# The tile loop of an encoder kernel's front: order of the vector work, half-row copies a step later, list entries stored last

## The chip, the cores and the metric

The kernel runs on one core of a Trainium2 chip. The metric is the device time of one execution in microseconds; the number of a kernel is the median of its runs. The profile is one further execution, read with the hardware profiler.

## What is computed

The reference is one layer of a streaming encoder, for 1024 prompt tokens and 64 sample tokens of width 1024. What matters here is its beginning:

```
m = silu(c) @ w_ada + b_ada                 # (6 * 1024) values for each of 2 conditions
sh1, sc1, g1, sh2, sc2, g2 = split(m, 6)
h = rmsnorm(x, norm_mix) * (1 + sc1) + sh1  # 1088 x 1024
qa, ka, va, fa, qb, kb, vb = split(h @ w_in)
logf = log_sigmoid(fa + b_f)                # fa: 8 columns, the forget gates
```

Then come two groups of attention heads, an output projection, a router (top group, top two experts in it), 32 experts and a final norm. `w_ada` is 1024 x 6144, 24 MB; all of it has to be read for the two vectors `c` of the conditions.

## The kernel before

The kernel is a row of blocks: the front (`modulate_in`), attention, the output projection with the router, and the experts. In a block each engine runs an instruction list of its own, written out by hand; engines wait for each other by semaphores, and every engine has to leave a block before any enters the next. So the front lasts as long as its slowest engine.

**What the front does.** It cuts `w_ada` into 12 halves of 512 columns (2 MB each), numbered 0 to 11. It handles halves 0 to 8, and attention 9 to 11. Halves 0 to 3 give the shift and scale that the front itself needs; they come ahead of the tile loop. A half takes three steps: TensorE multiplies it by the two condition vectors (`partial_rows`, L244; the prediction calls it the product), ScalarE copies the result out of PSUM (`modulation_out`, L380), and TensorE sums and transposes the copy into columns (`summed_columns`, L448; "sums"). Two PSUM banks and two copies take turns: product n waits for the copy of n-2, and copy n waits for the sums of n-2.

**The tile loop.** The tokens are 9 tiles (eight of 128 and one of 64). For a tile t:
- ScalarE squares and sums the rows (`square`, L373), VectorE scales the sum (`mean_square`, L520), GpSimd raises it to the power -1/2 (L350), VectorE multiplies the rows by it (`normalise`, L525)
- TensorE transposes the tile, 8 transposes (`transpose_x`, L459)
- ScalarE (L389) and VectorE (L534) each `move` four of the eight blocks out of PSUM, with shift and scale applied
- ScalarE rounds the result to the high half (`upper`, L397), and VectorE takes what is left as the low half (`lower`, L542). Two buffers `h` take turns, so the moves of tile t wait for the lower of t-2

The transposes run two tiles ahead of the moves, the normalisation three, the squares four. In turn t of the loop TensorE also does a product (half 4 in turn 2, up to half 8 in turn 6) and the sums of the half of the turn before, and ScalarE copies that turn's product in the same turn, behind the square.

**The forget gates.** The columns of `fa` are made in three chunks of tokens, 0 to 383, 384 to 767 and 768 to 1087: `gate_part` (16 matmuls, L470) after turns 4 and 7 and at the end, a copy by ScalarE (L404), `gate_sum` (L477), and the logits with the bias on VectorE (L557, L555). One PSUM bank serves all three.

**Loads.** SP issues everything on one queue. Three halves have homes; half n waits until the product of the half that was last in its home is done. So half 7 waits for product 4, half 8 for product 5, half 9 for 6 and half 10 for 7. Behind half 6 SP also issues the first weights of attention (`raw`, L334) and the two stores that fill the router's list of entries with "no entry" (L337, L338), taken from `far`, the last of nine rows of a buffer. SP waits for these stores at the end of its block. GpSimd splits the raw weights into two halves (L354, L356) at the end of its list.

Of the kernel before, what the change touches and what calls it, by code (L numbers as in the profile page):

```python
# [25 lines left out]
P = 128  # L26
D = 1024
# [125 lines left out]
def build(nc, a, o):  # L153
    with ExitStack() as ctx:
# [35 lines left out]
        with ExitStack() as c0:  # L190
            both = Scope(nc, c0, "both")
            k["wide"] = both.sb("wide", [P, 4 * BAND])
            k["w_ld"] = [both.sem(f"w_ld{j}") for j in range(HELD)]
            k["mrow_ready"], k["mrow_out"] = both.sem("mrow_ready"), both.sem("mrow_out")
            k["mod_ready"], k["mod_out"] = both.sem("mod_ready"), both.sem("mod_out")
            with ExitStack() as c:  # L196
                s = Scope(nc, c, "in")
                modulate_in(nc, s, a, o, k, hT, w_split)
                k["past"] = s.sems
            with ExitStack() as c:  # L200
                attention(nc, Scope(nc, c, "att"), a, o, k, hT, w_split)
# [46 lines left out]
def modulate_in(nc, s, a, o, k, hT, w_split):  # L248
# [1 line left out]
    h_hi, h_lo = hT  # L250
    TILES = NT + 1
    AHEAD = 3
    X_FIRST = False
    w_ada = [k["rows_all"][:, 4 * j:4 * j + 4, :].rearrange("p t (a n) -> p (t a) n", a=2) for j in range(2)]
    w_ada += [s.sb("w_ada", [P, NC, D // 2])[:, :, :]]
    far = k["rows_all"][:, NT, :].bitcast(I32)
# [21 lines left out]
    sq_done, ms_done, rstd_done, xn_done = s.sem("sq_done"), s.sem("ms_done"), s.sem("rstd_done"), s.sem("xn_done")  # L278
    xT_ready, xT_out_act, xT_out_dve = s.sem("xT_ready"), s.sem("xT_out_act"), s.sem("xT_out_dve")
    hi_done, lo_done, wf_split = s.sem("hi_done"), s.sem("lo_done"), s.sem("wf_split")  # L280
    half_set, far_set, sc_clear, far_stored = s.sem("half_set"), s.sem("far_set"), s.sem("sc_clear"), s.sem("far_stored")
    f_ready, f_moved, f_summed, z_done = s.sem("f_ready"), s.sem("f_moved"), s.sem("f_summed"), s.sem("z_done")
    own_dve, w_hi_done, w_lo_done = s.sem("own_dve"), s.sem("w_hi_done"), s.sem("w_lo_done")
    xp, xs = a["x_prompt"][0], a["x_sample"][0]
    block = s.ctx.enter_context(nc.Block())
    FIRST = 4

    def halves_at(t):

        n = FIRST + t - 2  # L290
        return [n] if FIRST <= n < min(EARLY, HALVES - HELD) else []

    IN_LOOP = sum(len(halves_at(t)) for t in range(TILES))

    def chunk_ending(t):

# [2 lines left out]
    @block.sync  # L299
    def _(sp):  # L300
        def load_half(n):
            sp.dma_start(w_ada[W_HOME[n]], a["w_ada"][n]).then_inc(w_ld[W_HOME[n]], 16)

        def load_x(t):
            sp.dma_start(x[0:rows_of(t), t, :], xs if t == NT else xp[t * P:t * P + P, :]).then_inc(x_ld[t], 16)

        sp.dma_start(vecs[:, :], a["vecs"]).then_inc(vec_ld, 16)
        if X_FIRST:
            for t in range(2):
                load_x(t)  # L310
            sp.dma_start(consts[:, :], a["consts"][:, 0:K_END]).then_inc(c_ld, 16)
            for t in range(2, TILES):
                load_x(t)
            for n in range(HELD):
                load_half(n)
        else:
            load_half(0)
            sp.dma_start(consts[:, :], a["consts"][:, 0:K_END]).then_inc(c_ld, 16)
            for n in range(1, HELD):
                load_half(n)  # L320
            for t in range(3):
                load_x(t)
        for n in range(HELD, min(EARLY + 2, HALVES)):
            sp.wait_ge(mrow_ready, last_in_home(n) + 1)
            load_half(n)
            if n == HELD and not X_FIRST:
                for t in range(3, TILES):
                    load_x(t)
            if n == 4:
                sp.dma_start(w_f[:, :, :], a["w_f"]).then_inc(wf_ld, 16)  # L330
                sp.dma_start(b_f[:, :], a["b_f"]).then_inc(wf_ld, 16)
            if n == 6:
                sp.wait_ge(xT_ready, 3)
                sp.dma_start(raw, a["w_qkv"][0].rearrange("b p k n -> p b k n")).then_inc(raw_ld, 16)  # L334
                sp.wait_ge(far_set, 1)
                entries = k["lists"].rearrange("(p n) c -> p (n c)", p=P)
                sp.dma_start(entries[:, 0:D], far).then_inc(far_stored, 16)  # L337
                sp.dma_start(entries[:, D:LISTS // P * 4], far[:, 0:LISTS // P * 4 - D]).then_inc(far_stored, 16)  # L338
        sp.wait_ge(far_stored, 32)

    @block.gpsimd
    def _(pool):
# [17 lines left out]
    def _(act):  # L360
# [5 lines left out]
        def square(t):  # L366
            r = rows_of(t)
            m = min(t, NT - 1)
            unused = h_lo[0:r, :, m * P:m * P + P]
            if t == NT:  # L370
                act.wait_ge(sq_done, NT)
            act.wait_ge(x_ld[t], 16)
            act.activation(unused, x[0:r, t, :].rearrange("p (c n) -> p c n", c=NC), ACT.Square,  # L373
                           accum_out=ssq[0:r, t:t + 1]).then_inc(sq_done, 1)
# [28 lines left out]
                act.wait_ge(f_summed, c)  # L403
            act.activation(f_parts[:, 0:hi - lo], f_ps[:, 0:hi - lo], ACT.Copy).then_inc(f_moved, 1)  # L404

        if X_FIRST:
            for t in range(TILES):
                square(t)
            for n in range(FIRST):
                modulation_out(n)  # L410
        else:
            for n in range(FIRST - 1):
                modulation_out(n)
            for t in range(AHEAD):
                square(t)
            modulation_out(FIRST - 1)
            square(AHEAD)
        act.wait_ge(a1_done, 1)
        for t in range(TILES):
            move(t)  # L420
            upper(t)
            if t + AHEAD + 1 < TILES and not X_FIRST:
                square(t + AHEAD + 1)
            if t == 2:
                act.wait_ge(wf_ld, 32)
                act.activation(w_f_parts[:, :, 0:8], w_f[:, :, :], ACT.Copy).then_inc(wf_split, 1)
            for n in halves_at(t):
                modulation_out(n)
            if chunk_ending(t - 1) is not None:
                gate_rows_out(chunk_ending(t - 1))  # L430
        for n in range(FIRST + IN_LOOP, EARLY):
            modulation_out(n)
        gate_rows_out(2)

# [1 line left out]
    def _(pe):  # L436
# [25 lines left out]
        def gate_part(c):  # L462
            lo, hi = CHUNKS[c]
            pe.wait_ge(wf_split, 2)
            pe.wait_ge(lo_done, (hi + P - 1) // P)
            if c:
                pe.wait_ge(z_done, c)
            for i, part in enumerate((h_hi, h_lo)):
                for kc in range(NC):
                    ins = pe.matmul(f_ps[0:16, 0:hi - lo], w_f_parts[:, kc, :], part[:, kc, lo:hi],  # L470
                                    start=(i == 0 and kc == 0), stop=(i == 1 and kc == NC - 1))
            ins.then_inc(f_ready, 1)

        def gate_sum(c):
# [4 lines left out]

        pe.wait_ge(c_ld, 16)  # L480
        pe.wait_ge(silu_done, 1)
        if X_FIRST:
            transpose_x(0)
            transpose_x(1)
        partial_rows(0)
        for n in range(1, FIRST):
            if n == FIRST - 1 and not X_FIRST:
                transpose_x(0)
                transpose_x(1)
            partial_rows(n)  # L490
            summed_columns(n - 1)
        summed_columns(FIRST - 1)
        pe.wait_ge(a1_done, 1)
        for t in range(TILES):
            if t + 2 < TILES:
                transpose_x(t + 2)
            for n in halves_at(t):
                partial_rows(n)
            if chunk_ending(t - 1) is not None:
                gate_sum(chunk_ending(t - 1))  # L500
            for n in halves_at(t - 1):
                summed_columns(n)
            if chunk_ending(t) is not None:
                gate_part(chunk_ending(t))
        for n in halves_at(NT):
            summed_columns(n)
        for n in range(FIRST + IN_LOOP, EARLY):
            partial_rows(n)
            summed_columns(n)
        gate_part(2)  # L510
        gate_sum(2)
# [2 lines left out]
    def _(dve):  # L514
# [41 lines left out]
            end = min(hi, SEQ)  # L556
            dve.tensor_scalar(z[:, lo:end], f_ps[0:8, 0:end - lo], b_f[:, 0:1], None, ALU.add).then_inc(z_done, 1)  # L557

        ready = TILES if X_FIRST else AHEAD
        mean_square(0)  # L560
        for t in range(ready):
            if t + 1 < TILES:
                mean_square(t + 1)
            normalise(t)
# [4 lines left out]
        dve.wait_ge(a1_done, 1)  # L569
        for t in range(TILES):  # L570
            move(t)
            if t + ready < TILES:
                if t + ready + 1 < TILES:
                    mean_square(t + ready + 1)
                normalise(t + ready)
            if t:
                lower(t - 1)
            if t == 3:
                dve.wait_ge(wf_split, 1)
                dve.tensor_tensor(w_f_parts[:, :, 8:16], w_f[:, :, :], w_f_parts[:, :, 0:8], ALU.subtract)\  # L580
                   .then_inc(wf_split, 1)
            if t >= 2 and chunk_ending(t - 2) is not None:
                logits(chunk_ending(t - 2))
# [34 lines left out]
def attention(nc, s, a, o, k, hT, w_parts):  # L618
# [473 lines left out]
    def _(dve):  # L1092
# [124 lines left out]
        for n in range(ALL):  # L1217
            for at in range(TILES):
# [9 lines left out]
                if at == 1 and n + 1 < ALL:  # L1228
                    cache_lower(n + 1)
                    if n == 0:  # L1230
                        dve.wait_ge(pT_ready, turn["gates"] + 1)
                        dve.tensor_copy(gate_rows, pT_ps[turn["gates"] % 2][0:GATE_ROWS, 0, :]).then_inc(pT_out, 1)
                t, r, _, _, u = tile(n, at)
# [1052 lines left out]
```

## Time and profile before

| | us |
|---|---|
| median of 3 runs | 1245.49 |
| the runs | 1245.49, 1238.99, 1247.1 |
| the profiled execution | 1240.19 |
| its span, first to last instruction | 1238.4 |
| TensorE busy | 1100.7 (89%) |
| VectorE busy | 491.6 (40%) |
| ScalarE busy | 356.3 (29%) |
| GpSimd busy | 366.4 (30%) |
| mean granted clock of TensorE | 0.955 |

PE is TensorE's matmuls, PEld its weight loads, DVE VectorE, ACT ScalarE, POOL GpSimd, SP the queue engine. The page divides the span into 40 slices of 31 us; the front is the first two and nearly all of the third. In a timeline a row is one instruction or several of a line run together: start, duration, engine, line, operation, what it writes and reads, how many, and in brackets how long the engine had been idle before it and what ended that.

### The profile page before, as it was taken

What the parts mean: (1) busy time and instruction counts of PE and PEld (TensorE: products, weight loads), DVE (VectorE), ACT (ScalarE), POOL (GpSimd) and SP (SyncE); (2) the same over time, 40 slices, a digit from 0 to 9 for tenths busy, and PEclk for the clock granted to TensorE, in tenths of its full rate; (3) what the DMA queues carried; (4) which work ended last, traced back from release to release, by engine and by line L of the source; (5) the groups of instructions that cost most, each with busy time, mean ns of one, the idle gap of its engine ahead of it and who ended that gap; (6) DMA issues with size and microseconds to landing.
All of it is one profiled execution on the core that took longest, in us unless ns stands there. A gap on an engine that the chain in (4) does not pass through costs nothing. (4 is left out here: it accounts for less than half of the span.)

```text
span 1238.4 us, 20082 instructions
## 1 busy us (share of the span) xinstructions
PE 1100.7 (89%) x7180; PEld 767.1 (62%) x7180; DVE 491.6 (40%) x1307; ACT 356.3 (29%) x1130; POOL 366.4 (30%) x306
## 2 busy tenths in 40 slices
PE   5589999999999899999986899962999999989956
PEld 2348788888888788888875688851333333333322
DVE  0453344444444344453555267754111212111227
ACT  2643334434334334433454122210111111011102
POOL 1150633535353403113033144435222222121001
PEclk8799999999999999999999899975999999999978
DMA  9953323223141504021077511125999999999784
GB/s 382 404 196 110 96 69 108 93 64 101 62 118 34 166 1 120 14 72 45 1 221 212 188 69 69 69 103 215 398 374 373 413 414 393 406 368 422 281 306 158
DMA packets 86809, 238.63 MB, mean 193 GB/s; under 512 B 10456, under 2 KB 58024, under 8 KB 75952
## 3 DMA queue, kind: packets, MB, share of 16 engines
q1 hardware_dynamic: 68384, 132.01, 30.5%
q10 hardware_dynamic: 7344, 78.91, 15.8%
q0 software_dynamic: 10976, 26.32, 5.7%
q8 instruction: 65, 1.06, 0.3%
q14 instruction: 40, 0.33, 0.1%
HBM read 208.19 MB, written 38.45 MB: 199 GB/s over the span
## 5 line engine op out<-in xcount | busy, mean ns | idle before, releaser
L1987 PE MATMUL moe_gu_ps<-a_gu,moe_xT_sb 128*64 x416 | 185.1, 598 | 5.2 <-DMA b_gu<-in_w_gu 3.3
L942 PE MATMUL att_piece_ps<-hT_hi,w_hi 128*128 128x384 f32 (+1 forms) x528 | 184.4, 349 | 2.4 <-PEq L196 1.0
L1990 PE MATMUL moe_gu_ps<-b_gu,moe_xT_sb 128*64 128x512 f32 x416 | 185.1, 598 | 0.0
L942 PE MATMUL att_piece_ps<-hT_hi,w_lo 128*128 128x384 f32 (+1 forms) x528 | 172.7, 327 | 0.0
L942 PE MATMUL att_piece_ps<-hT_lo,w_hi 128*128 128x384 f32 (+1 forms) x528 | 172.5, 327 | 0.0
L1167 DVE COPY att_pT_sb<-att_pT_ps 128x512 f32<-128x512 f32 (+2 forms) x192 | 94.6, 520 | 133.4 <-PE att_pT_ps L1010 132.9
L1987 PEld LDWEIGHTS moe_gu_ps<-a_gu,moe_xT_sb 128*64 128x64 f32 x416 | 57.0, 138 | 125.7 <-issue 125.7
L1271 ACT ACTIVATE att_probs_sb<-att_probs_sb,att_nmax_sb 128x640 f32<-128x640 f32 (+5 forms) x144 | 101.4, 704 | 41.3 <-DVE att_nmax_sb L1153 40.6
L1289 ACT ACTIVATE keep_rows_all_sb<-att_o_ps,att_rden_sb 128x64 f32<-128x64 f32 x144 | 37.3, 310 | 246.8 <-PE att_o_ps L1031 246.8
L942 PEld LDWEIGHTS att_piece_ps<-hT_hi,w_hi 128*128 128x128 f32 x528 | 99.1, 188 | 11.1 <-issue 6.0
L1153 DVE CUSTOM_DVE_ANT_0 att_probs_sb<-att_s_ps,both_wide_sb 128x640 f32<-128x640 f32 (+5 forms) x144 | 95.3, 662 | 26.8 <-PE att_s_ps L998 15.0
L2010 PE MATMUL moe_y_ps<-a_dn,moe_hT_sb 128*64 x208 | 94.8, 598 | 5.4 <-DVE moe_hT_sb L2156 4.7
L942 PEld LDWEIGHTS att_piece_ps<-hT_lo,w_hi 128*128 128x128 f32 x528 | 99.5, 188 | 0.0
L942 PEld LDWEIGHTS att_piece_ps<-hT_hi,w_lo 128*128 128x128 f32 x528 | 99.1, 188 | 0.0
L2013 PE MATMUL moe_y_ps<-b_dn,moe_hT_sb 128*64 128x512 f32 x208 | 94.8, 598 | 0.0
L1010 PE MATMUL att_pT_ps<-keep_consts_sb,att_probs_sb 128*128 128x128 f32 (+2 forms) x560 | 87.7, 278 | 1.8 <-ACT att_probs_sb L1271 1.7
L907 POOL CAST w_hi<-att_w_raw_sb 128x1024 fp32r<-128x1024 f32 x21 | 21.8, 1039 | 212.2 <-PE att_piece_ps L942 173.6
L1025 PE MATMUL att_o_ps<-att_pT_sb,att_v_rows_sb 128*64 128x128 f32 (+1 forms) x1088 | 74.4, 277 | 7.7 <-DVE att_pT_sb L1167 6.5
L1931 POOL DMA_INDIRECT x<-h_rows,moe_entries_sb x26 | 25.8, 993 | 161.6 <-DMA moe_entries_sb<-lists,route_at_sb 75.5
L1010 PEld LDWEIGHTS att_pT_ps<-keep_consts_sb,att_probs_sb 128*128 128x128 f32 (+2 forms) x560 | 62.7, 139 | 16.9 <-issue 11.6
L1025 PEld LDWEIGHTS att_o_ps<-att_pT_sb,att_v_rows_sb 128*64 128x64 f32 (+1 forms) x1088 | 58.1, 136 | 23.2 <-issue 13.2
L2073 ACT ACTIVATE moe_xT_sb<-moe_xT_ps 128x512 f32<-128x512 f32 x26 | 15.5, 598 | 187.9 <-PE moe_xT_ps L1976 183.7
(312 smaller groups left out, 1964.1 us busy)
## 6 DMA issues: line engine op xcount, KB each, us to landing
b_gu<-in_w_gu ACTq DMA_DIRECT2D x25, 2048.0 KB
b_dn<-in_w_dn ACTq DMA_DIRECT2D x25, 1024.0 KB
a_gu<-in_w_gu SPq DMA_DIRECT2D x10, 2048.0 KB
keep_rows_all_sb<-in_w_ada SPq DMA_DIRECT2D x9, 2048.0 KB, 11.2
att_w_raw_sb<-in_w_qkv SPq DMA_DIRECT2D x21, 512.0 KB, 3.7
a_dn<-in_w_dn SPq DMA_DIRECT2D x10, 1024.0 KB
w_out_parts<-keep_rows_all_sb SPq DMA_DIRECT2D x16, 512.0 KB, 4.8
in_w_ada_sb<-in_w_ada SPq DMA_DIRECT2D x3, 2048.0 KB, 16.6
```

The source lines that it names most:

```text
L942: ins = pe.matmul(bank[:, 0:hi - lo], w[:, kind, kc, :], x[:, kc, lo:hi], start=(m == 0), stop=(m == 3 * NC - 1))
L1010: ins = pe.transpose(pT_ps[e % 2][0:m, b - b0, 0:r], probs[h][0:r, b * P:b * P + m], ident[0:r, 0:r])
L1025: ins = pe.matmul(o_ps[head, 0:r], v, pT[h][0:m, b, 0:r], start=(b == 0), stop=(b == len(kb) - 1))
L1153: dve.tensor_tensor_reduce(probs[h][0:r, 0:wide], s_ps[h][0:r, 0:wide], bias, -SCALE, BIG, ALU.add, ALU.min, nmax[0:r, 2 * at + h:2 * at + ...
L1167: ins = dve.tensor_copy(pT[h][:, b0:b1, :], pT_ps[e % 2][:, 0:b1 - b0, :])
L1271: act.activation(probs[h][0:r, 0:wide], probs[h][0:r, 0:wide], ACT.Exp, bias=nmax[0:r, 2 * at + h:2 * at + h + 1], scale=-1.0, accum_out=d ...
L1289: ins = act.activation(rows_all[0:r, t, first + HD * h:first + HD * h + HD], o_ps[0:r, P + HD * h:P + HD * h + HD], ACT.Copy, scale=rden[0 ...
L1931: pool.indirect_dma_start(x[p % 3][:, :], None, k["h2"], bass.IndirectOffsetOnAxis(ap=entry[:, p, 0:1], axis=0), bounds_check=TOK - 1, oob ...
L1987: pe.matmul(gu_ps[p % 2][LANE[0], :], xT[:, c, LANE[0]], a_gu[:, bass.ds(slot, 1), c, :].rearrange("p a n -> p (a n)"), start=(c == 0), st ...
L1990: ins = pe.matmul(gu_ps[p % 2][LANE[1], :], xT[:, c, LANE[1]], b_gu[p % 3][:, c, :], start=(c == 0), stop=(c == NC - 1))
L2010: pe.matmul(y_ps[LANE[0], half], hT[:, c, LANE[0]], a_dn[:, bass.ds(slot, 1), c, half].rearrange("p a n -> p (a n)"), start=(c == 0), stop ...
L2013: ins = pe.matmul(y_ps[LANE[1], half], hT[:, c, LANE[1]], b_dn[p % 2][:, c, half], start=(c == 0), stop=(c == 1))
```

## The change

- VectorE's order in a turn is now moves, lower, normalise, mean square; it was moves, mean square, normalise, lower.
- The products of halves 4 to 8 are in turns 2, 3, 4, 6 and 8 (they were in 2 to 6). ScalarE copies a product in the turn after it, and TensorE makes the sums in the turn after that (in a turn, before gate part and gate sum).
- SP issues the stores of the list entries at the end of its list, behind half 10, and no longer waits for them. VectorE waits for them in attention, before it overwrites a part of that row.
- The last gate part is two sets of 16 matmuls, over tokens 768 to 1023 and 1024 to 1087, the first without a wait for the lower of the last tile.
- A branch for another order of loads, switched off by a constant, is removed.

```diff
@@ modulate_in
+    HALF_AT = {2: 4, 3: 5, 4: 6, 6: 7, 8: 8}
     def halves_at(t):
-        n = FIRST + t - 2
-        return [n] if FIRST <= n < min(EARLY, HALVES - HELD) else []
-    IN_LOOP = sum(len(halves_at(t)) for t in range(TILES))
+        return [HALF_AT[t]] if t in HALF_AT else []
@@ SP, inside "if n == 6" before, behind the loop after
-                sp.wait_ge(far_set, 1)
-                entries = k["lists"].rearrange("(p n) c -> p (n c)", p=P)
-                sp.dma_start(entries[:, 0:D], far).then_inc(far_stored, 16)
-                sp.dma_start(entries[:, D:LISTS // P * 4], far[:, 0:LISTS // P * 4 - D]).then_inc(far_stored, 16)
-        sp.wait_ge(far_stored, 32)
+        sp.wait_ge(far_set, 1)
+        entries = k["lists"].rearrange("(p n) c -> p (n c)", p=P)
+        sp.dma_start(entries[:, 0:D], far).then_inc(k["far_stored"], 16)
+        sp.dma_start(entries[:, D:LISTS // P * 4], far[:, 0:LISTS // P * 4 - D]).then_inc(k["far_stored"], 16)
@@ ACT
         for t in range(TILES):
             move(t)
             upper(t)
-            if t + AHEAD + 1 < TILES and not X_FIRST:
+            if t + AHEAD + 1 < TILES:
                 square(t + AHEAD + 1)
...
-            for n in halves_at(t):
+            for n in halves_at(t - 1):
                 modulation_out(n)
             if chunk_ending(t - 1) is not None:
                 gate_rows_out(chunk_ending(t - 1))
-        for n in range(FIRST + IN_LOOP, EARLY):
+        for n in halves_at(TILES - 1):
             modulation_out(n)
         gate_rows_out(2)
@@ PE, gate_part(c)
             pe.wait_ge(wf_split, 2)
-            pe.wait_ge(lo_done, (hi + P - 1) // P)
             if c:
                 pe.wait_ge(z_done, c)
-            for i, part in enumerate((h_hi, h_lo)):
-                for kc in range(NC):
-                    ins = pe.matmul(f_ps[0:16, 0:hi - lo], w_f_parts[:, kc, :], part[:, kc, lo:hi],
-                                    start=(i == 0 and kc == 0), stop=(i == 1 and kc == NC - 1))
+            for n0, n1 in [(lo, min(hi, SEQ))] + [(SEQ, hi)] * (hi > SEQ):
+                pe.wait_ge(lo_done, (n1 + P - 1) // P)
+                for i, part in enumerate((h_hi, h_lo)):
+                    for kc in range(NC):
+                        ins = pe.matmul(f_ps[0:16, n0 - lo:n1 - lo], w_f_parts[:, kc, :], part[:, kc, n0:n1],
+                                        start=(i == 0 and kc == 0), stop=(i == 1 and kc == NC - 1))
@@ PE, the loop
                 transpose_x(t + 2)
             for n in halves_at(t):
                 partial_rows(n)
-            if chunk_ending(t - 1) is not None:
-                gate_sum(chunk_ending(t - 1))
-            for n in halves_at(t - 1):
+            for n in halves_at(t - 2):
                 summed_columns(n)
             if chunk_ending(t) is not None:
                 gate_part(chunk_ending(t))
-        for n in halves_at(NT):
-            summed_columns(n)
-        for n in range(FIRST + IN_LOOP, EARLY):
-            partial_rows(n)
+            if chunk_ending(t - 1) is not None:
+                gate_sum(chunk_ending(t - 1))
+        for n in halves_at(TILES - 2) + halves_at(TILES - 1):
             summed_columns(n)
         gate_part(2)
         gate_sum(2)
@@ DVE, the loop
             move(t)
-            if t + ready < TILES:
-                if t + ready + 1 < TILES:
-                    mean_square(t + ready + 1)
-                normalise(t + ready)
             if t:
                 lower(t - 1)
+            if t + AHEAD < TILES:
+                normalise(t + AHEAD)
+            if t + AHEAD + 1 < TILES:
+                mean_square(t + AHEAD + 1)
@@ attention, DVE, pair 0, second tile
                     if n == 0:
+                        dve.wait_ge(k["far_stored"], 32)
                         dve.wait_ge(pT_ready, turn["gates"] + 1)
                         dve.tensor_copy(gate_rows, pT_ps[turn["gates"] % 2][0:GATE_ROWS, 0, :]).then_inc(pT_out, 1)
```

## Rows read from the trace of the kernel before

**Rows 1.** Page, 40 slices of the span: granted clock in tenths.
```profile
PEclk8799999999999999999999899975999999999978
```
**Rows 2.** Timeline of PE, the seam to attention: start, duration, idle before.
```profile
90.00 0.42 PE L942 MATMUL att_piece_ps<-hT_hi,w_hi 128*128 128x384 f32 x1 [1.02 <-PEq L196]
```
**Rows 3.** Waits, 30 to 92 us: total, times, longest.
```profile
ACT both_wide_sb L380 <- PE in_row_ps L244: 20.7, 6, 5.7
```
**Rows 4.** Timeline of ACT, turn 3 of the tile loop.
```profile
51.84 1.50 ACT L389 ACTIVATE in_h_sb<-in_xT_ps,keep_mod_sb,in_a_sb 128x128 f32<-128x128 f32 x4
53.37 1.06 ACT L397 ACTIVATE hT_hi<-in_h_sb 128x1024 fp32r<-128x1024 f32 x1
54.34 1.04 ACT L373 ACTIVATE hT_lo<-in_x_sb 128x1024 fp32r<-128x1024 f32 x1
...
58.07 0.60 ACT L380 ACTIVATE both_wide_sb<-in_row_ps 128x512 f32<-128x512 f32 x1 [2.60 <-PE in_row_ps L244]
```
**Rows 5.** Timeline of PE, 46 to 88 us.
```profile
46.30 1.94 PE L459 MATMUL in_xT_ps<-keep_consts_sb,in_x_sb 128*128 128x128 f32 x8 [3.79 <-ACT in_h_sb L389]
...
53.44 1.42 PE L459 MATMUL in_xT_ps<-keep_consts_sb,in_x_sb 128*128 128x128 f32 x8 [2.17 <-ACT in_h_sb L389]
54.79 3.20 PE L244 MATMUL in_row_ps<-in_w_ada_sb,both_wide_sb 128*32 128x512 f32 x16
...
65.56 1.55 PE L470 MATMUL in_f_ps<-hT_hi,in_w_f_parts_sb 128*16 128x384 f32 x8
...
68.35 1.03 PE L459 MATMUL in_xT_ps<-keep_consts_sb,in_x_sb 128*128 128x128 f32 x8
69.31 1.92 PE L244 MATMUL in_row_ps<-keep_rows_all_sb,both_wide_sb 128*32 128x512 f32 x16
72.31 0.81 PE L477 MATMUL in_f_ps<-in_f_parts_sb,keep_consts_sb 16*8 16x384 f32 x2 [1.08 <-ACT in_f_parts_sb L404]
73.05 1.05 PE L448 MATMUL in_mod_ps<-keep_consts_sb,both_wide_sb 128*128 128x2 f32 x8
74.03 0.82 PE L459 MATMUL in_xT_ps<-keep_consts_sb,in_x_sb 64*128 64x64 f32 x8
74.78 3.44 PE L244 MATMUL in_row_ps<-in_w_ada_sb,both_wide_sb 128*32 128x512 f32 x16
...
86.43 1.34 PE L470 MATMUL in_f_ps<-hT_lo,in_w_f_parts_sb 128*16 128x320 f32 x8
```
**Rows 6.** Timeline of DVE: first moves, a lower, a normalise, the last logits.
```profile
34.66 1.37 DVE L534 TENSOR_SCALAR in_h_sb<-in_xT_ps,in_a_sb,keep_mod_sb 128x128 f32<-128x128 f32 x4
...
49.09 1.22 DVE L542 TENSOR_TENSOR hT_lo<-in_h_sb,hT_hi 128x1024 fp32r<-128x1024 f32 x1
...
55.58 0.74 DVE L525 TENSOR_SCALAR in_x_sb<-in_x_sb,in_rstd_sb 128x1024 f32<-128x1024 f32 x1
...
89.22 0.46 DVE L557 TENSOR_SCALAR both_wide_sb<-in_f_ps,in_b_f_sb 8x256 f32<-8x256 f32 x1
```
**Rows 7.** DMA issues at 17.6, 24.4, 31.8, 38.4, 51.3 us: KB, us to landing.
```profile
keep_rows_all_sb<-in_w_ada SPq DMA_DIRECT2D x1, 2048.0 KB, 24.9
...
in_w_ada_sb<-in_w_ada SPq DMA_DIRECT2D x1, 2048.0 KB, 23.2
...
keep_rows_all_sb<-in_w_ada SPq DMA_DIRECT2D x1, 2048.0 KB, 20.6
...
lists<-keep_rows_all_sb SPq DMA_DIRECT2D x1, 512.0 KB, 17.9
...
keep_rows_all_sb<-in_w_ada SPq DMA_DIRECT2D x1, 2048.0 KB, 11.2
```
**Rows 8.** Windows: PE, PEld, DVE, ACT, POOL busy; clock, DMA share, GB/s.
```profile
76.00:77.00 1.00, 1.00 (x8) 0.20 (x4) 0.89 (x4) 0.00 (x0) 1.00 (x1) 0.50 1.00 426
...
84.00:86.00 2.00, 1.21 (x8) 1.00 0.00 0
```
**Rows 9.** Timeline of DVE in attention, the copy behind the new wait.
```profile
152.05 0.27 DVE L1232 COPY keep_rows_all_sb<-att_pT_ps 64x128 f32<-64x128 f32 x1
```

More of the change, by code:

```diff
@@ L194, in build @@
             k["mrow_ready"], k["mrow_out"] = both.sem("mrow_ready"), both.sem("mrow_out")
-            k["mod_ready"], k["mod_out"] = both.sem("mod_ready"), both.sem("mod_out")
+            k["mod_ready"], k["mod_out"], k["far_stored"] = both.sem("mod_ready"), both.sem("mod_out"), both.sem("far_stored")
             with ExitStack() as c:
@@ L252, in modulate_in @@
     AHEAD = 3
-    X_FIRST = False
     w_ada = [k["rows_all"][:, 4 * j:4 * j + 4, :].rearrange("p t (a n) -> p (t a) n", a=2) for j in range(2)]
@@ L280, in modulate_in @@
     hi_done, lo_done, wf_split = s.sem("hi_done"), s.sem("lo_done"), s.sem("wf_split")
-    half_set, far_set, sc_clear, far_stored = s.sem("half_set"), s.sem("far_set"), s.sem("sc_clear"), s.sem("far_stored")
+    half_set, far_set, sc_clear = s.sem("half_set"), s.sem("far_set"), s.sem("sc_clear")
     f_ready, f_moved, f_summed, z_done = s.sem("f_ready"), s.sem("f_moved"), s.sem("f_summed"), s.sem("z_done")
@@ L307, in _ @@
         sp.dma_start(vecs[:, :], a["vecs"]).then_inc(vec_ld, 16)
[L308 to L322, printed above, removed]
+        load_half(0)
+        sp.dma_start(consts[:, :], a["consts"][:, 0:K_END]).then_inc(c_ld, 16)
+        for n in range(1, HELD):
+            load_half(n)
+        for t in range(3):
+            load_x(t)
         for n in range(HELD, min(EARLY + 2, HALVES)):
@@ L325, in _ @@
             load_half(n)
-            if n == HELD and not X_FIRST:
+            if n == HELD:
                 for t in range(3, TILES):
@@ L404, in gate_rows_out @@
             act.activation(f_parts[:, 0:hi - lo], f_ps[:, 0:hi - lo], ACT.Copy).then_inc(f_moved, 1)
[L406 to L417, printed above, removed]
+        for n in range(FIRST - 1):
+            modulation_out(n)
+        for t in range(AHEAD):
+            square(t)
+        modulation_out(FIRST - 1)
+        square(AHEAD)
         act.wait_ge(a1_done, 1)
@@ L481, in _ @@
         pe.wait_ge(silu_done, 1)
-        if X_FIRST:
-            transpose_x(0)
-            transpose_x(1)
         partial_rows(0)
         for n in range(1, FIRST):
-            if n == FIRST - 1 and not X_FIRST:
+            if n == FIRST - 1:
                 transpose_x(0)
@@ L557, in logits @@
             dve.tensor_scalar(z[:, lo:end], f_ps[0:8, 0:end - lo], b_f[:, 0:1], None, ALU.add).then_inc(z_done, 1)
-        ready = TILES if X_FIRST else AHEAD
         mean_square(0)
-        for t in range(ready):
+        for t in range(AHEAD):
             if t + 1 < TILES:
```

## The prediction

> **What bounds the kernel now.** The page first: the span is 1238.4 us, and the front is its first two to three slices of 31 us, the ones where TensorE was granted 0.8, 0.7 and 0.9 of its clock [rows 1]. The timeline of PE at the seam gives its end: attention's first matmul is at 90.00 us, once every engine has left the front's block [rows 2]. The change touches only what lies before that, so the question is how early 90.00 can come.
>
> The waits of 30 to 92 us say who is late there. ScalarE waits six times, 20.7 us in all, for PE's half-row products (L380 on L244) [rows 3], and TensorE idles 3.79 us before the transposes of tile 4 until ScalarE's move is done [rows 5]. Neither is slow; they wait for each other. The timeline of ACT shows the cycle: move of a tile 1.50 us, high half (upper) 1.06, square 1.04 and its read, then 2.60 us idle until PE's product exists, the copy of it 0.60 (0.5 before the next can start), and only then the next move, although that tile's transpose had long been there [rows 4]. On PE: transposes 1.42, product of a half 3.20, sums 1.05 [rows 5]. One turn is move 1.5, transposes 1.4, product 3.2, copy 0.5, handovers 0.1: 6.7 us, and from tile 2 to tile 7 it is paid each time. VectorE is not the limit: moves 1.37, lower 1.22, normalise 0.74 make 3.3 us a tile [rows 6].
>
> **The change, part by part.** I write the new order out by the waits in the code, with those durations, from 34.66 us, where both moves of tile 0 start [rows 6] and nothing ahead is touched. The same was done for the old order as a control: it comes out at 89.9 us for the last VectorE instruction, against 89.22 + 0.46 = 89.7 in the trace [rows 6].
>
> *Lower directly behind the moves.* Old, the lower of tile t-1 stood behind the scaled square sum and the normalisation, which wait for ScalarE's square. The old ACT move of tile 2 waited for it. New, a step is: upper 1.0, square 1.1, sum 0.1, VectorE's moves 1.3, handover: 3.6 to 3.7 us. ACT's move of tile 2 ends at 43.4 and PE's transposes of tile 4 run 43.5 to 45.4 (1.94 us [rows 5]). Old they started at 46.3. Gain here: about 2.7 us. The normalisation of tile t+3 comes later in its step, but is still 2 us or more ahead of its transpose. The square sum is last; it holds only the next moves, as it did before.
>
> *Copies a step later.* ScalarE now does the next move before it waits for the product, so move and product lie side by side. From 45.4 PE no longer waits for anybody; it becomes the bound: product 4 to 48.6, transposes 5 to 50.0, product 5 to 53.2, transposes 6 to 54.6, product 6 to 57.8, sums 4 to 58.8, gate part 0 (16 matmuls, two blocks of 1.55 that overlap: 3.0) to 61.8, transposes 7 (1.0) to 62.8, sums 5 to 63.8, gate sum 0 to 64.5, transposes 8 to 65.3, product 7 (1.9) to 67.2, sums 6 to 68.2, gate part 1 to 71.2, product 8 (3.4) to 74.6, sums 7 to 75.6, gate sum 1 to 76.3, sums 8 to 77.3 [rows 5]. ACT waits for gate part 0 before its move of tile 6 (62.2 to 63.7), and transposes 8 need that move: 0.8 us to spare, the tightest place. VectorE ends the lower of tile 8 at about 70.5.
>
> *The tail.* VectorE adds the bias rows (0.2) after sums 8 and makes logits 1 (0.6): 78.1. Gate part 2 waits for that, as before. Split, it is 16 matmuls of 256 columns and 16 of 64. Eight of 384 take 1.55 and eight of 320 take 1.34 [rows 5], so 64 columns are worth about 0.2: eight of 256 about 1.1, sixteen 2.1. For sixteen of 64 columns no row exists: between 0.8 (the slope) and 2.1 (no gain at all from being short); I take 1.0, near the slope. Together 3.1 against the 2.5 or so of two unsplit blocks: the split costs 0.6 us, and gives nothing, because the lower of tile 8 is done 7 us before. Then the ACT copy 0.4, gate sum 0.7 and logits 0.7: 83.2. The seam costs 0.3 as before (89.7 to 90.0): attention starts at 83.5 instead of 90.0. **6.5 us gained.**
>
> *SP and the loads.* Landings from issue [rows 7]: half 4 at 17.6 + 24.9 = 42.5, half 6 at 31.8 + 20.6 = 52.4, the list entries at 38.4 + 17.9 = 56.2, half 7 at 51.3 + 11.2 = 62.5. Half 5, at 24.4 + 23.2, is between: 47.5. Products 4, 5 and 6 start at 45.4, 50.0 and 54.6, so each has 2.2 to 3 us to spare. Half 7 is issued when product 4 is done (48.6 instead of 51.3). The 0.55 MB of entries, worth 1.3 us at 426 GB/s, as the loads run [rows 8], are no longer ahead of it: it lands at about 60.7, and is wanted at 65.3. Half 8 follows 5 us later (65.7, wanted at 71.2). The entries are now behind half 10, which is issued at 67.2 and lands by 76; they follow by 78, with the queue empty until 83.5. SP leaves its block without waiting for them. VectorE's new wait stands before the copy at 152.05 [rows 9], some 70 us after; cost nothing. Behind it on VectorE are reciprocals and the next pieces, so if the entries were late, all of attention would stop. GpSimd begins its split of the raw weights earlier (56 instead of 64.5), and needs 14 us: 70, covered.
>
> *The dead branch for the other load order* was never run: nothing.
>
> **Sum.** Profiled execution 1240.19 us (span 1238.4 and 1.8 around it) minus 6.5 is 1233.7. The three runs give 1238.99, 1245.49 and 1247.1, so the profiled one is 5.3 us under their median. The median less 6.5 is 1239.0. The two levels occur about equally often, so I take the middle, 1237. Attention's PE is busy nearly throughout and nothing in it is timed from the start of the program, so I expect the 6.5 us to arrive at the end undiminished.
>
> **The clock** is where my sum is weakest. Product 8 took 3.44 us and product 7 1.92 for the same work [rows 5]. At 76 to 77 us the granted clock is 0.50 (1.2 GHz) with PE busy 1.00 [rows 8]; before that PE had done sums of 2 columns and 64-column transposes, after a gap of 1.08 us [rows 5]. So in this trace a busy PE was slowed, and I left products 4, 5, 6 and 8 at the slow price.
> The Trainium skill (page "TensorE: Matmul & The Clock Gate", the clock-gate part) says that half rate is the state after idleness and full rate that after sustained activity. By it an unbroken PE from 43.5 on would run products 5, 6 and 8 at about 1.9 us, and the front would end at 79.2 and not 83.2. The 0.50 in a busy stretch speaks against taking that rule whole.
>
> **Rivals.**
> 1. *Full clock from product 5 on.* The mechanism is in this kernel: PE's gaps before the transposes, 3.79 us in the row of tile 4 [rows 5], go away, and the three products fall from 3.2 to 3.4 to 1.9. That is 1.3 + 1.3 + 1.5, on PE's unbroken chain: 4.0 more, less what half 6 at 52.4 may hold back. The gain is 10.5, the time 1229.7 to 1235. For: products 3 to 8 vary just so. Against: the row above. Chance 0.15.
> 2. *Half clock all through* (the slower side). From transposes 6 on, the chain is 28 us of PE. If the short matmuls kept the clock at 1.2 GHz there, products 7 would cost 1.4 more, five groups of sums 0.8 each, the gate parts 3.0, 3.0 and 3.1, transposes and gate sums 3: about 19 us, so the front would end at 102: 12.5 later than now, 1252.7 to 1258. It decides from about 6.5 us of such loss on. Against: the trace shows 0.50 for single stretches only, and 1.00 at 84 to 86 with PE busy 1.21 us of 2 [rows 8]. Chance 0.03.
> 3. *The time is given back.* PE stays bound by ACT at the gate rows: the copy of gate part 0 stands on ACT before the move of tile 6, so each delay of PE reaches the move and comes back to PE at transposes 8. With 0.8 us to spare, a product one clock step slower there is paid in full, and VectorE's lower, 1.2 us alone, stretches beside GpSimd's split. Gain 0 to 3 us: 1237 to 1245. Chance 0.14.
> 4. The forecast, gain 4 to 9 us: 0.68.
>
> **Numbers.** 1% is 12.4 us, about what can be told from no change here. The forecast gain is half that, so *same* holds most: 0.87. Faster needs rival 1 together with the lower level of the runs: 0.10. Slower: 0.03. The range: 1230.5 (the low level, gain 8.5) to 1243.5 (the high level, gain 2 to 3), which leaves out rival 2 and the ends of 1 and 3.
>
> **What would show it.** In the timeline of PE, products 4, 5 and 6 at about 45, 50 and 55 us with no idle from the transposes of tile 4 to sums 6; ACT's idle before L380 mostly gone; attention's first matmul at 83.5 (81 to 86). Gate part 2 in two blocks, 3.1 us. The entries' store landing near 78. The clock in the stretch 53 to 75. I am wrong if that first matmul is under 81 or over 87, or if the time between it and the end differs from 1148.4 us by more than 3.

## The result, and the profile after

The changed kernel takes 1231.46 us (median of 7 runs, 1230.81 to 1234.2), the kernel before 1241.63 beside it (7 runs, 1238.99 to 1247.54): ratio 0.991, interval 0.9889 to 0.9931. The time is inside the range of 1230.5 to 1243.5, at its lower edge, and 5.5 under the 1237 of the sum; the gain is 10.2 us where 6.5 were forecast.

The profiled execution (1234.2 us, one of the two longest of the seven) has a span of 1232.4. Two lines of its page, the span and the granted clock, to be read against [rows 1]:

```profile
span 1232.4 us, 20113 instructions
...
PEclk8789999999999999999998999975999999999978
```

The timeline of PE through the tile loop, rows as in [rows 5]:

```profile
43.48 1.94 PE L441 MATMUL in_xT_ps<-keep_consts_sb,in_x_sb 128*128 128x128 f32 x8 [1.73 <-DVE in_h_sb L511]
45.35 3.12 PE L244 MATMUL in_row_ps<-keep_rows_all_sb,both_wide_sb 128*32 128x512 f32 x16
48.41 1.09 PE L441 MATMUL in_xT_ps<-keep_consts_sb,in_x_sb 128*128 128x128 f32 x8
49.43 1.92 PE L244 MATMUL in_row_ps<-in_w_ada_sb,both_wide_sb 128*32 128x512 f32 x16
51.28 1.09 PE L441 MATMUL in_xT_ps<-keep_consts_sb,in_x_sb 128*128 128x128 f32 x8
52.31 1.92 PE L244 MATMUL in_row_ps<-keep_rows_all_sb,both_wide_sb 128*32 128x512 f32 x16
...
55.08 1.56 PE L453 MATMUL in_f_ps<-hT_hi,in_w_f_parts_sb 128*16 128x384 f32 x8
...
60.99 1.92 PE L244 MATMUL in_row_ps<-keep_rows_all_sb,both_wide_sb 128*32 128x512 f32 x16
...
66.64 1.92 PE L244 MATMUL in_row_ps<-in_w_ada_sb,both_wide_sb 128*32 128x512 f32 x16
...
72.12 1.86 PE L453 MATMUL in_f_ps<-hT_hi,in_w_f_parts_sb 128*16 128x256 f32 x8 [0.85 <-issue]
...
78.23 0.41 PE L918 MATMUL att_piece_ps<-hT_hi,w_hi 128*128 128x384 f32 x1 [1.03 <-PEq L196]
```

From 43.48 to 71.3 PE has no idle time worth a bracket. Transposes 4 start at 43.48, as worked out (43.5), and product 4 still takes 3.12 us. But products 5, 6 and 8 take 1.92 each; the forecast had 3.2, 3.2 and 3.4. Attention's first matmul is at 78.23 instead of 90.00 [rows 2]: 11.8 us earlier, not 6.5. The prediction had said what would show it wrong: a first matmul under 81, or a time from it to the end more than 3 us off 1148.4. Both came: 78.23, and 1232.4 - 78.23 = 1154.2.

ScalarE idled 2.60 us before the copy in the rows shown [rows 4], and 2.6 to 3.6 before each of the five. Now the copies of halves 4 to 7 come without a wait, and only that of half 8 waits 1.40 us (timeline of ACT, the copy at the end of turn 3 and the start of turn 4):

```profile
49.11 0.58 ACT L368 ACTIVATE both_wide_sb<-in_row_ps 128x512 f32<-128x512 f32 x1
49.59 1.50 ACT L377 ACTIVATE in_h_sb<-in_xT_ps,keep_mod_sb,in_a_sb 128x128 f32<-128x128 f32 x4
51.12 1.06 ACT L385 ACTIVATE hT_hi<-in_h_sb 128x1024 fp32r<-128x1024 f32 x1
```

The issues of SP at 48.5 and 51.4 us (half 7 and half 8), with the time to landing, as in [rows 7]:

```profile
keep_rows_all_sb<-in_w_ada SPq DMA_DIRECT2D x1, 2048.0 KB, 12.3
...
in_w_ada_sb<-in_w_ada SPq DMA_DIRECT2D x1, 2048.0 KB, 14.4
```

They land at 60.8 and 65.8 (forecast 60.7 and 65.7). Product 7 starts at 60.99, 0.2 us behind its half. TensorE got so much faster that it now runs level with the loads: a half 7 that lands any later holds it up.

**Of the 11.8 us, 6.0 arrive at the end of this execution** (1238.4 against 1232.4). VectorE's instructions in attention are the same ones in the same order in both kernels, so their distance can be followed: 10.2 us at 89 us of the changed kernel, 8.7 from 134 on, 7.4 from 440 on. Those are three steps of 1.3 to 1.6 us; smaller ones take the rest, among them two places where the clock is lower than before over the same work (mean 0.83 against 0.87 in the 40 us from 655, 0.72 against 0.77 in the 30 us from 1170; in the kernel before, from 664 and 1178). Windows of the changed kernel at those three places (columns: PE, PEld, DVE, ACT, POOL busy, clock, DMA share, GB/s):

```profile
80.00:82.00 2.00, 2.00 (x8) 2.00 (x8) 0.00 (x0) 1.06 (x2) 0.00 (x0) 0.51 0.39 128
130.00:132.00 2.00, 2.00 (x10) 1.78 (x11) 0.61 (x3) 0.60 (x2) 0.00 (x0) 0.50 0.87 238
420.00:422.00 2.00, 2.00 (x8) 2.00 (x7) 0.02 (x1) 0.10 (x2) 2.00 (x2) 0.50 0.00 0
```

At each, PE is fully busy at half clock, within 1 us behind a gap. The gaps are there in both kernels: 1.03 us at the seam (1.02 before), 1.70 at 129.5 (1.70) and 2.55 at 419 (2.78), and in the kernel before the clock stayed at 1.00 behind all three. The one at 129.5 is this, in the changed kernel and then in the one before:

```profile
129.52 0.33 PE L986 MATMUL att_pT_ps<-keep_consts_sb,att_probs_sb 128*128 128x128 f32 x1 [1.70 <-ACT att_probs_sb L1248]
```
```profile
139.75 0.33 PE L1010 MATMUL att_pT_ps<-keep_consts_sb,att_probs_sb 128*128 128x128 f32 x1 [1.70 <-ACT att_probs_sb L1271]
```

and the window behind the latter (PE busy, clock, DMA share, GB/s):

```profile
140.00:142.00 2.00, 2.00 (x15) 1.00 0.79 193
```

The same idle 1.70 us was followed by half clock once and not the other time. Twelve profiles stand in this document, and the program behind the front is the same in all but for one wait of VectorE. From attention's first matmul to the end they take 1148.2 to 1155.3 us: 1148.4 in the kernel before, 1154.2 and 1152.9 in two profiles of the changed one. So a difference of 6 us there is within what single executions differ by; over 7 runs each, the medians differ by 10.2 us.

### The profile page after: what moved, and what is told of

It reads as the page before. It is cut to its first block and busy times, and to the rows that moved or that the text cites. A ratio compares the mean times of both kernels' runs of the same rounds, so it can differ in the third digit from the quotient of the medians.

```text
span 1232.4 us, 20113 instructions
## 1 busy us (share of the span) xinstructions
PE 1102.8 (89%) x7196; PEld 772.9 (63%) x7196; DVE 492.3 (40%) x1307; ACT 355.8 (29%) x1130; POOL 363.6 (30%) x306
```

## The experiments

The measure of the front is attention's first matmul in the profile: before 90.0, changed 78.2. Each label names its edit.

**VectorE's order alone**, on the kernel before:

```diff
             move(t)
-            if t + ready < TILES:
-                if t + ready + 1 < TILES:
-                    mean_square(t + ready + 1)
-                normalise(t + ready)
             if t:
                 lower(t - 1)
+            if t + ready < TILES:
+                normalise(t + ready)
+            if t + ready + 1 < TILES:
+                mean_square(t + ready + 1)
```

> The kernel before with VectorE's new order alone (moves, lower, normalise, mean square). Attention's first matmul is the measure: 90.0 us in the kernel before, 78.2 in the changed one, a gain of 11.8. Theory A (two waits in series: each part alone leaves the other one on the path): the cycle of ScalarE and TensorE by the copy in the same turn stays, so the step of turns 3 to 6 stays at about 6.7 us, only turns 1 and 2 get shorter; first matmul at 87 (86 to 88), TensorE's clock still 0.5 in several stretches of 35 to 75 us. Rival B (the parts add up, and the order of the vector work is the larger one): 83 or earlier.

Measured: first matmul 87.34; ratio 0.9974 (0.9945 to 1.0003), not to be told from no change. The timeline of PE, turns 3 and 4:

```profile
50.77 1.43 PE L459 MATMUL in_xT_ps<-keep_consts_sb,in_x_sb 128*128 128x128 f32 x8 [2.17 <-issue]
52.13 3.20 PE L244 MATMUL in_row_ps<-in_w_ada_sb,both_wide_sb 128*32 128x512 f32 x16
...
57.50 1.32 PE L459 MATMUL in_xT_ps<-keep_consts_sb,in_x_sb 128*128 128x128 f32 x8 [1.19 <-issue]
58.75 3.29 PE L244 MATMUL in_row_ps<-keep_rows_all_sb,both_wide_sb 128*32 128x512 f32 x16
```

The step is 57.50 - 50.77 = 6.73, as before. The 2.7 us come from turns 1 and 2 alone, as the prediction had it.

**The copies alone** (products in turns 2, 3, 4, 6, 8; copies one turn, sums two turns later), on the kernel before:

```diff
+    HALF_AT = {2: 4, 3: 5, 4: 6, 6: 7, 8: 8}
...
@@ ACT
-            for n in halves_at(t):
+            for n in halves_at(t - 1):
                 modulation_out(n)
...
@@ PE
-            for n in halves_at(t - 1):
+            for n in halves_at(t - 2):
                 summed_columns(n)
...
```

> The kernel before with copies a step later, products in turns 2, 3, 4, 6 and 8 and the sums two turns later, but VectorE's old order, the list entries behind the raw weights and the last gate part in one piece. Theory A: ScalarE's moves now wait for the lower, which stands behind square sum and normalisation; written out by the waits this gives a first matmul at 87.5 at the half-clock prices of the kernel before and 84.5 at full clock. Rival B (this part is nearly all of it, by TensorE's unbroken work and its full clock): 79 to 80.

Measured: first matmul 84.81, in an execution whose tile loop began 1.4 us earlier in the span (transposes 2 at 35.03 against 36.4), so 86.2 on the scale of the others; ratio 0.9966 (0.9942 to 0.999). Product 5 is already at full clock here. The row of transposes 6 shows what is left: ScalarE's move is late, which waits for the lower.

```profile
50.62 1.06 PE L460 MATMUL in_xT_ps<-keep_consts_sb,in_x_sb 128*128 128x128 f32 x8 [0.73 <-ACT in_h_sb L390]
51.61 1.92 PE L244 MATMUL in_row_ps<-in_w_ada_sb,both_wide_sb 128*32 128x512 f32 x16
56.33 1.94 PE L460 MATMUL in_xT_ps<-keep_consts_sb,in_x_sb 128*128 128x128 f32 x8 [2.80 <-ACT in_h_sb L390]
58.20 2.52 PE L244 MATMUL in_row_ps<-keep_rows_all_sb,both_wide_sb 128*32 128x512 f32 x16
```

Alone the two parts bring 2.7 and 3.8 us in these profiles, and the whole change, with the entries moved as well, 11.8. That isn't yet a proof that they are worth more together. With both of them and the entries at their old place (below), the first matmul is at 83.97: 6.0 us earlier, no more than the sum of 6.5. And full clock doesn't need both: with the copies alone products 5, 7 and 8 took 1.92 us, product 5 behind a gap of 0.73, and only product 6, behind one of 2.80, took 2.52. The runs add up too: 0.3% for the order, 0.3% for the copies, 0.7% for both with the entries early, 0.9% for all, each uncertain by about 0.3%.

**Products in turns 2 to 6 again**, on the changed kernel:

```diff
-    HALF_AT = {2: 4, 3: 5, 4: 6, 6: 7, 8: 8}
+    HALF_AT = {2: 4, 3: 5, 4: 6, 5: 7, 6: 8}
```

> The changed kernel with the products of halves 4 to 8 in turns 2 to 6 again; the copies stay a step later. Theory A (the loads have become the bound: in the changed kernel product 7 starts at 60.99 with half 7 landed at 60.8): product 7 in turn 5 has to wait for its half until 60.8 with sums, gate sum and transposes behind it on TensorE, and product 8 until 65.8; first matmul at 80.8, 2.6 later than the changed kernel's 78.2. Rival (spreading is idle, the copy a step later is all): 78.2 as the changed kernel.

Measured: first matmul 79.49; ratio 0.9961 (0.9932 to 0.9989), 1230.76 to 1243.55 over 10 runs. The timeline of PE, and one long window of it (PE busy, clock, DMA share, GB/s):

```profile
60.96 1.92 PE L244 MATMUL in_row_ps<-keep_rows_all_sb,both_wide_sb 128*32 128x512 f32 x16 [1.93 <-DMA keep_rows_all_sb<-in_w_ada]
...
65.86 1.92 PE L244 MATMUL in_row_ps<-in_w_ada_sb,both_wide_sb 128*32 128x512 f32 x16 [0.61 <-DMA in_w_ada_sb<-in_w_ada]
...
74.73 1.09 PE L453 MATMUL in_f_ps<-hT_hi,in_w_f_parts_sb 128*16 128x256 f32 x8 [0.75 <-issue]
```
```profile
47.00:92.00 45.00, 39.78 (x295) 1.00 0.72 287
```

Both waits for loads are there; the loss is 1.3 us and not 2.6, since the last gate part ran at full clock here. A wait of 1.93 us right before product 7, the longest for a half in any profile here, cost no clock: it is 1.00 from 47 to 92 us. This profile is of the fastest run; with waits before the products the runs spread over 13 us, where the changed kernel's spread over 3.4 and 3.8. The slower runs have the lower mean clock over the whole program: 0.958 for the two runs at 1231 us, 0.948 to 0.952 for the six above 1237. So the clock has a part in the spread; whether it is lost in the front isn't shown, as no slower run was profiled.

**The entries behind the raw weights again**, on the changed kernel:

```diff
                 sp.dma_start(raw, ...).then_inc(raw_ld, 16)
-        sp.wait_ge(far_set, 1)
...
+                sp.wait_ge(far_set, 1)
...
+                sp.dma_start(entries[:, 0:D], far).then_inc(k["far_stored"], 16)
+                sp.dma_start(entries[:, D:LISTS // P * 4], ...).then_inc(k["far_stored"], 16)
```

> The changed kernel with the stores of the list entries issued behind the raw weights again (SP still doesn't wait for them). Theory A (loads bound product 7): half 7 lands 1.3 us later, product 7 starts about 1.2 us later, the first matmul is at 79.4 instead of 78.2. Rival (the entries are cover, as the prediction had it with 4 us of slack): 78.2, no change.

Measured: first matmul 83.97; ratio 0.9934 (0.9908 to 0.996). The timeline of PE, and one window of it (busy, clock, DMA share, GB/s):

```profile
62.36 3.64 PE L244 MATMUL in_row_ps<-keep_rows_all_sb,both_wide_sb 128*32 128x512 f32 x16 [1.25 <-DMA keep_rows_all_sb<-in_w_ada]
65.93 1.87 PE L430 MATMUL in_mod_ps<-keep_consts_sb,both_wide_sb 128*128 128x2 f32 x8
67.66 2.72 PE L453 MATMUL in_f_ps<-hT_hi,in_w_f_parts_sb 128*16 128x384 f32 x8
```
```profile
64.00:66.00 2.00, 2.00 (x13) 0.50 1.02 434
```

The load's delay is what was expected, 1.25 us. But product 7, the sums and most of gate part 1 behind it then ran at half clock: 5.7 us later in all. Both theories missed this. The wait alone doesn't explain it. In the kernel with products in turns 2 to 6, product 7 waited 1.93 us and stayed at full clock, and in the kernel with the last gate part in one piece (below) product 6 did so behind this wait:

```profile
52.27 1.92 PE L244 MATMUL in_row_ps<-keep_rows_all_sb,both_wide_sb 128*32 128x512 f32 x16 [1.29 <-DMA keep_rows_all_sb<-in_w_ada]
```

Over the runs this kernel is about 0.2% behind the changed one, within the intervals of both.

**The same, with the wait filled** by four useless matmuls ahead of product 7:

```diff
                 for n in halves_at(t):
+                    if n == 7:
+                        pe.wait_ge(mrow_out, n - 1)
+                        for _ in range(4):
+                            pe.matmul(row_ps[1][:, 0:384], ident, consts[:, 0:384], start=True, stop=True)
                     partial_rows(n)
```

> The kernel with the entries behind the raw weights (first matmul at 83.97, where product 7 waited 1.25 us for its half and then ran at half clock until about 72 us), with 4 useless matmuls of 384 columns put directly ahead of product 7, in the time in which it waits; they write a bank that product 7 overwrites. Theory A (the short gap, not the late load itself, costs most: it lets the clock fall): product 7 at full clock (1.9 us), first matmul at 79.5 to 80.0, 4 us or more earlier although work was added. Rival B (the clock fell by chance, or for the low use of the array by the sums): product 7 at 3.4 to 3.6 us as without them, first matmul at 84 or later.

The timeline of PE, and the same window:

```profile
61.04 2.85 PE L481 MATMUL in_row_ps<-keep_consts_sb 128*128 128x384 f32 x8
63.82 1.92 PE L244 MATMUL in_row_ps<-keep_rows_all_sb,both_wide_sb 128*32 128x512 f32 x16
```
```profile
64.00:66.00 2.00, 2.00 (x19) 1.00 0.96 410
```

Measured: first matmul 80.97. The fill was too long, product 7 started 1.5 us later than without it, and the front still ended 3.0 us earlier, at full clock until the last gate part. The ratio says less: 0.9945 (0.9919 to 0.9972), no better than unfilled. So one pair of profiles shows what the half clock cost, but not that the fill kept it away, since waits as long passed without it elsewhere, one of 1.53 us before product 6 in this same profile. The runs don't confirm a gain.

**The changed kernel again**, unedited:

> The changed kernel itself once more, beside the others. Theory A (TensorE's unbroken work from 43.5 us on holds the full clock up to the end of the front, so the front's end varies little; the stretches at half clock behind it fall where a sample hits a gap and differ from execution to execution): first matmul of attention at 78.2 plus or minus 0.5, runs again within about 5 us of each other, ratio 0.991 to 0.993. Rival (the profile of the first time was lucky in the front, and the rivals of the prediction at slow prices are as common): first matmul anywhere between 78 and 84.

Measured: 1233.05 us, ratio 0.9913 (0.9876 to 0.9951), runs 1231.97 to 1235.73. First matmul 79.62, 0.9 beyond the range expected and inside that of the rival. Products 5 to 8 take 1.92 or 1.93 again; in the timeline of PE the whole last gate part, its sum and the first matmuls of attention ran at half clock:

```profile
72.42 1.87 PE L453 MATMUL in_f_ps<-hT_hi,in_w_f_parts_sb 128*16 128x256 f32 x8 [0.85 <-issue]
74.09 1.91 PE L453 MATMUL in_f_ps<-hT_lo,in_w_f_parts_sb 128*16 128x256 f32 x8
```

**The last gate part in one piece**, on the changed kernel:

```diff
-            for n0, n1 in [(lo, min(hi, SEQ))] + [(SEQ, hi)] * (hi > SEQ):
+            for n0, n1 in [(lo, hi)]:
```

> The changed kernel with the last gate part in one piece (16 matmuls of 320 columns, waiting for the lower of the last tile, which is done 6 us before). Theory A: the split costs what it adds, 3.85 us in two pieces in the changed kernel against 2.5 to 2.7 in one; first matmul at 77.0 to 77.2, that is 1.0 to 1.2 earlier, if the clock is full there. Rival: the split's first piece starts earlier than one piece could, so undoing it costs: 78.5 or later.

Measured: first matmul 78.43; 1234.9 us, ratio 0.9926 (0.989 to 0.9961). Neither number was met, because here too most of the part fell into half clock (timeline of PE):

```profile
72.14 1.91 PE L453 MATMUL in_f_ps<-hT_hi,in_w_f_parts_sb 128*16 128x320 f32 x8 [0.85 <-issue]
73.86 2.33 PE L453 MATMUL in_f_ps<-hT_lo,in_w_f_parts_sb 128*16 128x320 f32 x8
```

At full clock the part takes 2.5 us split (the kernel with products in turns 2 to 6) and 2.5 in one (below). At half clock it takes 4.4 split (72.42 to 76.84, the kernel run again); the 4.05 in one can't be set against that, because its first 0.5 us were still at full clock. The split is worth nothing and costs nothing that shows.

**A denser end**, on the changed kernel with the gate part in one piece:

```diff
@@ PE
+            if t == NT:
+                gate_sum(1)
             for n in halves_at(t - 2):
                 summed_columns(n)
...
-            if chunk_ending(t - 1) is not None:
+            if chunk_ending(t - 1) is not None and t < NT:
                 gate_sum(chunk_ending(t - 1))
+        gate_part(2)
         for n in halves_at(TILES - 2) + halves_at(TILES - 1):
             summed_columns(n)
-        gate_part(2)
         gate_sum(2)
@@ DVE
+        logits(1)
         modulated(FIRST, EARLY).then_inc(k["mod_out"], 1)
-        logits(1)
         logits(2)
```

> The changed kernel with a denser end: gate sum 1 ahead of the sums of half 7, the last gate part in one piece and ahead of the sums of half 8, VectorE's logits 1 ahead of the bias rows. The waits of TensorE for VectorE (0.85) and for ScalarE's copy (0.5) then lie beside sums. Theory A (TensorE's own work is the bound behind product 8, which its load holds at 65.8): after product 8 (66.64 plus 1.9) come 0.7, 1.0, 2.6, 1.0 and 0.7 on TensorE and 0.7 on VectorE: first matmul at 75.5 (75 to 76.3), 2.7 earlier, of which half is the split. Rival (the wait moves on to ScalarE or to the logits): no better than the unsplit kernel, 77.0.

Measured: first matmul 75.19; 1228.17 us (4 runs, 1227.23 to 1229.88; the five runs of the changed kernel beside it are all above 1231.9), ratio to the kernel before 0.9863 (0.9827 to 0.99). Its slowest run is faster than the fastest of the twelve runs of the changed kernel (1230.81), so it beats both kernels. The timeline of PE from gate sum 1 on:

```profile
68.59 0.81 PE L460 MATMUL in_f_ps<-in_f_parts_sb,keep_consts_sb 16*8 16x384 f32 x2
69.33 1.05 PE L430 MATMUL in_mod_ps<-keep_consts_sb,both_wide_sb 128*128 128x2 f32 x8
70.24 1.33 PE L453 MATMUL in_f_ps<-hT_hi,in_w_f_parts_sb 128*16 128x320 f32 x8
71.42 1.33 PE L453 MATMUL in_f_ps<-hT_lo,in_w_f_parts_sb 128*16 128x320 f32 x8
```

The wait of 0.85 us ahead of the gate part is gone, and the part ran at full clock. That the wait was the cause isn't shown by this one profile. Of the seven profiles of a changed kernel with an idle 0.75 or 0.85 us there, six had half clock in some of the part and one had none; the kernel before, with 0.79, had none either.

**The idle time at the loop's start filled**, on the changed kernel:

```diff
+            if t < 3:
+                for _ in range(2):
+                    pe.matmul(row_ps[1][:, 0:384], ident, consts[:, 0:384], start=True, stop=True)
             if t + 2 < TILES:
                 transpose_x(t + 2)
```

> The changed kernel with two useless matmuls of 384 columns ahead of the transposes in each of turns 0, 1 and 2, where TensorE sits idle 1.5 to 2.8 us. If that brings the full clock earlier, product 4 takes 1.9 instead of 3.1 us and transposes 5 start 1.2 us earlier. Theory A (from product 7 on the loads are the bound; half 7 lands at 60.8 whatever TensorE does before): product 7 doesn't start before 60.8, first matmul at 78.0 to 78.5, no gain; and if the wait ahead of product 7 that opens costs the clock, 82 or later. Rival (TensorE's own work was the bound): first matmul at 77.0, 1.2 earlier.

Measured: 1232.28 us, ratio 0.9913 (0.9881 to 0.9946), the same as unfilled. Product 4 takes 1.92 and transposes 5 start at 47.29 instead of 48.41, and then, in the same timeline:

```profile
51.31 1.06 PE L441 MATMUL in_xT_ps<-keep_consts_sb,in_x_sb 128*128 128x128 f32 x8 [1.10 <-ACT in_h_sb L377]
52.45 1.92 PE L244 MATMUL in_row_ps<-keep_rows_all_sb,both_wide_sb 128*32 128x512 f32 x16
...
61.14 1.92 PE L244 MATMUL in_row_ps<-keep_rows_all_sb,both_wide_sb 128*32 128x512 f32 x16
```

The 1.1 us are given back before product 7: transposes 6 wait 1.10 us for ScalarE's move and start where they did (51.28), and half 6, issued at 31.9, takes 20.5 us and lands at 52.4, where product 6 starts. So product 7 is where it was (60.99), and its half, issued 2 us earlier than in the changed kernel, still lands only at 61.1. From product 6 on TensorE can't be earlier than the loads. The first matmul is at 79.62, again by half clock in the last gate part.

**Both**, the denser end and the filled start:

> Both: the denser end and the filled start. Theory A: first matmul at 75.2 as with the denser end alone (75.19), since half 7 sets product 7; the time no better than the denser end's 1228.2. Rival: 74.0.

Measured: 1228.93 us (8 runs), ratio 0.9899 (0.9872 to 0.9926): no better than the denser end alone. The first matmul was at 78.86, in an execution whose tile loop began 1.6 us later, and in which product 7 ran at half clock (3.59 us), behind transposes 8 and an idle 0.45 us before them. Filling the start doesn't protect the rest.

## Why the prediction was right or wrong

**The cycle of copy, move and transposes: right.** Transposes 4 were worked out at 43.5 (43.48), transposes 5 at 48.6 (48.41), with no idle after them. What the order does alone, 2.7 us, came out as forecast, and the step of 6.7 us stayed until the copies moved.

**The step that failed: "I left products 4, 5, 6 and 8 at the slow price".** Three of the four ran at full clock. Followed through the list, the measured start is earlier than the forecast one by 1.9 us at transposes 6, 3.6 at sums 4, 4.3 at product 7, 6.1 at sums 7; the products make up 4.0 of it, transposes 5 and 6 (1.09 against 1.4), the gate parts (2.8 against 3.0) and small roundings of the other terms the rest. The last gate part gave back 0.8, since it ran at half clock (3.9 us against 3.1). In all 5.3 us. The step went by rows of the kernel before, product 5 at 3.20 behind an idle 2.17 us and a busy TensorE at half clock at 76 us, and priced with them a stretch that had no gap at all. The row at 76 us came after sums, short transposes and a gap. What the runs showed in its place is the price, 1.92 us, in both profiles of the changed kernel. Why the clock is full there is shown only in part: it held through the unbroken stretch from 48.4 us on, but in other runs it also held with gaps.
Rival 1 had the front end at 79.2, attention at 79.5 and the time at 1229.7 to 1235; with 78.23 and 1231.46 it was the right case, and 0.15 was too little for it. That the time still fell in the stated range is the range's width and no merit of the sum: of the 5.5 us it was off, 3.7 are the gain, and the rest is that it took the kernel before at 1243.5 where seven runs gave 1241.63. The rule of the Trainium skill (page "TensorE: Matmul & The Clock Gate", the clock-gate part) that activity brings full rate and idleness half rate was the better guide: products 5 to 8 are at 1.92 us in the unbroken stretch in both profiles of the changed kernel, and 3.64 behind a wait of 1.25 us. Of short waits the traces don't agree on either answer: behind 1.29, 1.53 and 1.93 us a product took 1.92.

**The loads: landings right, conclusion wrong.** 60.8 and 65.8 were forecast to 0.1 us. But "wanted at 65.3" rested on the slow clock. Wanted at 61, half 7 is just in time, and moving the entries, which had 2.8 us to spare at the slow price (62.5 against 65.3), is worth 1.25 us of wait and in one profile 5.7 us. Over the runs it is about 0.2% (0.9934 against 0.991), less than the intervals.

**The split of the last gate part:** 0.6 us of cost was forecast; at full clock it is nothing (2.5 us either way). That it brings nothing was right.

**"I expect the 6.5 us to arrive undiminished": wrong for one execution.** 11.8 us became 6.0, 4.4 of it in three steps at half clock behind gaps that both kernels have. Over the medians it is 10.2 us.

**The wait for the entries in attention** costs nothing: the stores are issued at 63.4 and 63.8 and land 12 and 13 us later, the copy behind the wait is at 143.3.

**Slips in the sums.** The tail adds up to 83.0 and not 83.2, the middle of 1233.7 and 1239.0 is 1236.4 and not 1237, and the terms of rival 2 make 17.5 us and not 19. None of them changes what the prediction got right or wrong.

What stays open: why the same gap of 1.70 us in attention costs the clock in one execution and not in another, and so how much of the difference between two single profiles is the kernel's.

## What to carry to other kernels

Where two engines wait for each other in turn, write the new order out by the waits in the code: it gave the starts here to 0.2 us as long as the prices were right. Price a stretch that will be unbroken at the full clock's rows, and keep the slow ones for the slow end of the range; then look again at what was called slack, because a faster engine uses it up, and the next late transfer delays it and sometimes costs it the clock. When a seam moves by some microseconds, follow one engine's identical instructions behind it before the gain is booked at the end, and don't read a difference of some microseconds between two single profiles as the kernel's.

## What the runs showed of the hardware

- In one profile a wait of 1.25 us of TensorE for a load, ended at 62.4, was followed by half clock until about 71 us, with PE busy 2.00 of 2.00 in each 2 us from 64 to 70; with useless matmuls in its place the clock stayed at 1.00 until 74. In another, with waits of 1.93 and 0.61 us for loads, it stayed at 1.00 from 47 to 92. A busy TensorE can so run at half clock for 9 us, and a short wait by itself doesn't decide it.
- Half 7 was issued at 46.6, 47.9, 48.5 and 48.6 us in four kernels with the entries last, and landed between 60.9 and 61.3. Issued at 48.6 with the entries ahead of it, it landed at 62.3. Its landing went by what was ahead of it in the queue.
- The same 16 matmuls of a product took 1.92 us at full clock and 3.64 at a mean of 0.50. Those of 3.1 to 3.4 us ran in part at each: the mean clock over the 3.20 us of product 5 before was 0.59.
- Sixteen matmuls of 256 columns and sixteen of 64 take 2.5 us at full clock, as long as sixteen of 320.
